# Expert stage of a two-block network: six row buffers in place of eight, and the last six query weight tiles loaded into a buffer of their own at the stage's beginning

## The reference, cut to what matters

```python
q = (x @ w_query).reshape(T, HEADS, 256)          # x: 256 x 1024, w_query: 1024 x 2048
s1 = einsum('thd,nd->thn', q[..., :128], sub_keys1)
s2 = einsum('thd,nd->thn', q[..., 128:], sub_keys2)
v1, i1 = top_k(s1, 16); v2, i2 = top_k(s2, 16)
top_s, top_p = top_k(all sums v1 + v2, 16)        # 16 experts of each head and token
e_idx = i1[top_p // 16] * 128 + i2[top_p % 16]
gate = softmax(top_s)
u = expert_u[e_idx]; act = gelu(einsum('cd,ced->ce', x, u))
y = einsum('ce,ced->cd', gate * act, expert_v[e_idx])
```

## Time and profile before

| | |
|---|---|
| Median of three executions | 2153.61 us (2153.51 to 2156.51) |
| The profiled execution's own time | 2153.96 us |
| Its span in the profile | 2152.2 us |
| PE, DVE, ACT, POOL busy over the span | 86%, 69%, 48%, 20% |
| Gathers | 256, together 268.45 MB |
| HBM read over the span | 494.73 MB, 230 GB/s in the mean |
| DMA rate in slices 9 to 19 of 40 (about 430 to 1020 us) | 416 to 422 GB/s |

### The profile page before, as it was taken

The page is one execution under the profiler, slowest core; times in us unless marked ns, Lnnn a source line. Parts: engine busy times, 40 slices in busy tenths (PEclk is TensorE's granted clock), DMA queues, the critical chain, the costliest instruction groups (busy, mean ns, idle before and its releaser), DMA issues. The chain is left out here.

```text
span 2152.2 us, 33416 instructions
## 1 busy us (share of the span) xinstructions
PE 1860.4 (86%) x12148; PEld 1393.9 (65%) x12148; DVE 1486.2 (69%) x2618; ACT 1026.3 (48%) x2065; POOL 436.7 (20%) x457
## 2 busy tenths in 40 slices
PE   4974897998987877777899989889999999779998
PEld 4842887844432222222289988678998989668997
DVE  6676654787777677666466675766777787777666
ACT  2444212554554444444355554467665545435554
POOL 0010220144544434444200000002221331210000
PEclk8987998899999999999999999799999999889999
DMA  9860001599999999999855555035555555224553
GB/s 333 290 224 35 3 3 41 187 416 420 421 421 421 422 421 421 421 420 422 358 178 187 185 179 198 1 118 184 187 182 180 190 181 176 93 91 158 192 186 98
DMA packets 104385, 497.31 MB, mean 231 GB/s; under 512 B 11856, under 2 KB 17232, under 8 KB 71376
## 3 DMA queue, kind: packets, MB, share of 16 engines
q1 hardware_dynamic: 66064, 225.41, 31.2%
q0 software_dynamic: 36864, 268.45, 30.0%
q10 hardware_dynamic: 1344, 1.96, 0.3%
HBM read 494.73 MB, written 1.05 MB: 230 GB/s over the span
## 5 line engine op out<-in xcount | busy, mean ns | idle before, releaser
L247 PE MATMUL ps<-srcs,wh 128*128 128x512 f32 x2064 | 742.1, 401 | 23.2 <-DVE srcs L261 20.4
L1924 PE MATMUL ps<-row,diag 128*128 128x512 f32 x1024 | 498.2, 622 | 114.5 <-ACT diag L2028 114.3
L249 PE MATMUL ps<-srcs,wl 128*128 128x256 f32 x2064 | 583.2, 283 | 0.0
L229 DVE TENSOR_TENSOR wl<-ring,wh 128x1024 fp32r<-128x1024 f32 x362 | 452.3, 1252 | 120.0 <-ACT wh L223 118.7
L247 PEld LDWEIGHTS ps<-srcs,wh 128*128 128x128 f32 x2064 | 392.6, 190 | 115.3 <-issue 27.2
L1924 PEld LDWEIGHTS ps<-row,diag 128*128 128x128 f32 x1024 | 183.0, 193 | 417.5 <-ACT diag L2028 258.9
L2129 DVE CUSTOM_DVE_ANT_0 row<-row,h_tok 128x1024 f32<-128x1024 f32 x256 | 313.5, 1225 | 191.7 <-DMA row<-in_peer_uv,experts 178.9
L223 ACT ACTIVATE wh<-ring 128x1024 fp32r<-128x1024 f32 x362 | 379.2, 1051 | 65.4 <-PE ps L249 43.1
L249 PEld LDWEIGHTS ps<-srcs,wl 128*128 128x128 f32 x2064 | 395.4, 192 | 2.5 <-issue 2.4
L1837 POOL DMA_INDIRECT row<-in_peer_uv,experts x256 | 280.5, 1096 | 384.2 <-PE ps L1924 346.7
L2021 ACT ACTIVATE acts<-dots 128x1 f32<-128x1 f32 x256 | 51.8, 202 | 328.4 <-DVE dots L2129 327.7
(11 more groups left out here) (520 smaller groups left out, 2180.3 us busy)
## 6 DMA issues: line engine op xcount, KB each, us to landing
ring<-in_stream SPq DMA_DIRECT2D x378, 512.0 KB, 3.8
alpha<-in_ada_late SPq DMA_DIRECT2D x12, 512.0 KB, 5.8
beta<-in_ada_late SPq DMA_DIRECT2D x10, 512.0 KB, 5.8
kappa<-in_ada_late SPq DMA_DIRECT2D x10, 512.0 KB, 6.3
row<-in_peer_uv,experts POOLq DMA_INDIRECT x256
bias<-in_attn_bias SPq DMA_DIRECT2D x8, 256.0 KB, 5.2
w<-in_cmp_w SPq DMA_DIRECT2D x1, 2048.0 KB, 7.7
xT<-in_xT SPq DMA_DIRECT2D x1, 1024.0 KB, 15.4
```

The lines of the kernel that those rows point to most:

```text
L229: nc.vector.tensor_tensor(wl[:, n % PAIRS, :], ring[:, tile % RING, :], wh[:, n % PAIRS, :].bitcast(F32), ALU.subtract).then_inc(tiles_fre ...
L247: nc.tensor.matmul(out, wh[:, n, cols], source.rearrange("p a t -> p (a t)"), start=start, stop=stop, skip_group_check=True)
L249: return nc.tensor.matmul(out[:, 0:S], wl[:, n, cols], source[:, 0, :], start=False, stop=stop, skip_group_check=True)
L1924: last = nc.tensor.matmul(y_part(t, half), diag[:, s % DIAGS, :], row[:, s % ROWS, D + half * 512:D + (half + 1) * 512], start=(slot == 0) ...
```

## The change

Six row buffers instead of eight free 16 KB in each partition. A new buffer `extra` with six places takes 24 KB; the difference is made up by letting `weights` share its memory with `dots` and `whole` with `hot`. At the stage's beginning, right behind the subkeys, SP loads query tiles 10 to 15 into `extra`. `refill` then loads only query tiles 6 to 9 into the ring; the six ring slots that tiles 10 to 15 would have had are skipped (SP waits for the slot's earlier load and counts its semaphore up itself), and the next stage's first two tiles are loaded as before, when query tiles 10 and 11 have been split. ACT and DVE read tiles 10 to 15 from `extra`. POOL's wait in front of gather s is now for `v_used` of slot s - 6.

```diff
-        def high(act, tile, turns=0):
+        def high(act, tile, turns=0, held=None):
 
             n = split_no(tile)
-            act.wait_ge(loaded[tile % RING], turns * 16 + 16 * (tile // RING + 1))
+            source = held[0] if held else ring[:, tile % RING, :]
+            if held:
+                act.wait_ge(held[1], 16)
+            else:
+                act.wait_ge(loaded[tile % RING], turns * 16 + 16 * (tile // RING + 1))
             if n >= PAIRS:
                 act.wait_ge(tiles_used, turns * RING + (n - PAIRS + 1))
-            nc.scalar.activation(wh[:, n % PAIRS, :], ring[:, tile % RING, :], ACT.Copy).then_inc(high_done, 1)
+            nc.scalar.activation(wh[:, n % PAIRS, :], source, ACT.Copy).then_inc(high_done, 1)
...
-        ROWS = 8
+        ROWS = 6
...
+        EXTRA = RING
         row_in = [sem(f"row_in{i}") for i in range(ROWS)]
+        extra_in = [sem(f"extra_in{i}") for i in range(EXTRA)]
...
-            whole = sb("query_whole", [P, 2, S], where=tmp)
+            extra = sb("extra", [P, EXTRA, D], where=tmp)
...
-            dots, acts, weights = (sb(n, [P, TT * SLOTS], where=tmp) for n in ("dots", "acts", "weights"))
+            dots, acts = (sb(n, [P, TT * SLOTS], where=tmp) for n in ("dots", "acts"))
+            weights = dots
...
+            whole = hot[:, :, :, :].rearrange("p a b c -> p a (b c)")
...
+            def extra_at(n):
+                return (extra[:, n, :], extra_in[n]) if 0 <= n < EXTRA else None
...
                 sp.dma_start(subkeys[:, :, :], A["subkeys"]).then_inc(keys_in, 16)
-                refill(sp, first, T_QUERY - RING + AHEAD)
+                for i in range(EXTRA):
+                    sp.dma_start(extra[:, i, :], A["stream"][first + T_QUERY - EXTRA + i]).then_inc(extra_in[i], 16)
+                refill(sp, first, T_QUERY - EXTRA - RING)
+                for i in range(T_QUERY - EXTRA, T_QUERY):
+                    slot = (first + i) % RING
+                    sp.wait_ge(loaded[slot], 16 * ((first + i) // RING))
+                    sp.sem_inc(loaded[slot], 16)
+                refill(sp, first + T_QUERY - RING, AHEAD)
                 for s in range(TT * SLOTS - ROWS, TT * SLOTS):
                     sp.wait_ge(row_in[s % ROWS], 16 * (s // ROWS + 1))
                 refill(sp, first + T_QUERY - RING + AHEAD, RING - AHEAD)
...
                 def weight_and_copy(i):
-                    high(act, first + AHEAD + i)
+                    n = AHEAD + i - (T_QUERY - EXTRA)
+                    high(act, first + AHEAD + i, held=extra_at(n))
                     copy_low(i)
```

More of the change, by code:

```diff
@@ L215, in split_no, with low @@
             return tile - T_ADA
-        def high(act, tile, turns=0):
+        def high(act, tile, turns=0, held=None):
             n = split_no(tile)
-            act.wait_ge(loaded[tile % RING], turns * 16 + 16 * (tile // RING + 1))
+            source = held[0] if held else ring[:, tile % RING, :]
[3 more added lines that the diff above has]
+                act.wait_ge(loaded[tile % RING], turns * 16 + 16 * (tile // RING + 1))
             if n >= PAIRS:
                 act.wait_ge(tiles_used, turns * RING + (n - PAIRS + 1))
-            nc.scalar.activation(wh[:, n % PAIRS, :], ring[:, tile % RING, :], ACT.Copy).then_inc(high_done, 1)
-        def low(dve, tile, turns=0):
+            nc.scalar.activation(wh[:, n % PAIRS, :], source, ACT.Copy).then_inc(high_done, 1)
+        def low(dve, tile, turns=0, held=None):
             n = split_no(tile)
+            source = held[0] if held else ring[:, tile % RING, :]
             dve.wait_ge(high_done, turns * RING + (n + 1))
-            nc.vector.tensor_tensor(wl[:, n % PAIRS, :], ring[:, tile % RING, :],
+            nc.vector.tensor_tensor(wl[:, n % PAIRS, :], source,
                                     wh[:, n % PAIRS, :].bitcast(F32), ALU.subtract).then_inc(tiles_freed, 1)
@@ L2146, in weight @@
                 def weight(i):
-                    low(dve, first + AHEAD + i)
+                    n = AHEAD + i - (T_QUERY - EXTRA)
+                    low(dve, first + AHEAD + i, held=extra_at(n))
                 def out(i):
```

## The result

The changed kernel takes **2162.63 us** in the median of nine executions (2158.43 to 2168.7). The kernel before, executed beside it, takes 2155.88 us (nine executions, 2153.51 to 2157.18). The ratio is 1.0036, with a 95% interval of 1.0026 to 1.0046. The change makes the kernel slower by some 7 us, where +1.1 us was forecast, and the time lies above the range given. The profiled execution of the changed kernel took 2160.01 us, 6.05 us more than that of before.

A forecast was written before the change was run, and what follows sets the result against it. The gathers' bytes on the DMA engines bound the stage; -6.2 us of tiles against about 8 us of dry queue came by the landings to +1.1 us, others 0: 2154.7 us, own range 2153.3 to 2155.1, wider range 2151.5 to 2158.5.

The forecast's parts named there:

- The bound: Expert stage's gathers: length is its bytes at 421 GB/s while the slowest DMA engine's queue never runs empty.
- The tiles, -6.2 us: Query tiles 11 to 15 leave the saturated stretch, 5 x 1.245 = 6.2 us, and cost nothing at the stage's beginning.
- The dry stretch, some 8 us: Stage's start: six gathers queued run dry at 432.6 us, gather 6 is issued at 439.88; engines idle some 8 us.
- An unqueued gather: Time from the end of its issue to its landing with nothing queued: taken as 4.2 us, bounds 3.4 and 4.6.
- The start, +1.1 us: Landing of gather 19 at 477.8 us against 476.75 before, tiles included: +1.1 us, bounds -0.3 and +1.5.
- gather k is now issued where gather k + 2 was: Rule for following landings after the dry queue: issues shift by two gathers while the consumers keep their times.
- The steady part, 0 us: After the start, a turn of six buffers lasts 14.9 us instead of 19.9; the slowest engine doesn't run dry: 0 us.
- that leaves 2.9 us, against 0.9 us from issue to first data: Gather 55, the tightest found: issue ends at 564.26 us, slowest engine begins it at 567.2, so it isn't starved.
- One sign named in the forecast: Prediction is wrong if dots in heads 1 to 4 wait over 2.49 us for each other in the mean.
- The slower one: Six buffers don't cover the loop; five tight gathers starve if issue to first data exceeds 2.9 us: 2159.7 us, chance 0.13.
- The faster rival: Slot 0 finishes earlier, queue isn't dry, the whole 6.2 us are gained: 2147.4 us, chance 0.08.
- The base: Starting time for the sum: profiled execution of the kernel before, 2153.96 us, with the median shown 0.35 us lower.

The follow-up runs named there:

- second profiles: The changed kernel and the kernel before, each executed and profiled again with no edit: changed 2161.6 us, ratio 1.0033; before against itself 0.9998.
- run 4: The kernel before with six row buffers instead of eight and no tile moved: 2163.14 us, ratio 1.0031.
- six behind the start: The kernel before, eight buffers kept, but gathers from the 33rd on wait as if there were six; tiles in place: 2159.21 us, ratio 1.0010.
- four under way: The kernel before, eight buffers kept, but from slot 80 on gather s also waits for gather s - 4 to land: ratio 1.0009.
- run 7: The kernel before, eight buffers kept, with at most four, three or two gathers under way from slot 80 on: ratios 1.0009, 1.029, 1.0729.
- Six at the start: The kernel before, eight buffers kept, but the first 32 gathers wait as if there were six; tiles in place: 2159.18 us, ratio 1.0014.

## Why the prediction was wrong

**The bound.** Right: the stage lasts as long as its bytes when the queue is full. Eight buffers with two tiles moved gained what they should, and the slowest engine decides: the last landing is still behind the rest. The tail is steeper, as forecast. The end of the gathers in the changed kernel, to be read beside the earlier trace rows:

```profile
1072.00:1075.00 3.00, 2.50 (x6) 0.68 (x4) 1.48 (x4) 1.11 (x5) 0.00 (x0) 1.00 0.99 412
1075.00:1078.00 3.00, 2.27 (x5) 0.68 (x4) 1.23 (x2) 1.38 (x5) 0.00 (x0) 1.00 0.23 96
```

Some 6 to 3 us ahead of the last dot the share is still 0.99; before it was 0.17 at that distance. The lag between the first and the last of the 16 engines at gather 255 is 3.2 us instead of 7.9 (2.1 instead of 8.1 in the second profiles).

**The tiles, -6.2 us.** Right as bytes: they are gone, and at their new place they delay nothing (0.61 of the DMA share from 392 to 415 us instead of 0.36, and the first gather follows the subkeys' issue by 22.9 us as before, 22.8). With six buffers at most 2.8 us of them are seen by slot 31, and in the medians nothing (run 4).

**The dry stretch, some 8 us.** Right in place and nearly in size. POOL's seventh gather waits 13.91 us, for PE, and is issued 22.13 us behind the first, 23.25 us in the second profile; forecast was 23.3. The row of the changed kernel for three us ahead of it:

```profile
439.00:442.00 3.00, 3.00 (x9) 1.33 (x8) 2.93 (x12) 1.14 (x5) 0.94 (x1) 1.00 0.01 3
```

The share is 0.01. (Forecast were 433 to 441 us; the whole stage began 2.9 us later.) In the mean of the 16 engines, idle time from the first issue to the landing of slot 19 grew by 6.7 and 7.6 us in the two pairs of profiles. An unqueued gather takes 4.50 us (gather 0) and 4.52 us (gather 6) from the end of its issue to its landing, where I took 4.2 of 3.4 to 4.6; over all the profiles gather 0 takes 4.50 to 4.81 us. From the Trainium skill, page "DMA: Bandwidth & Descriptors", section "Anatomy of one DMA — SWDGE (gpsimd) path", an estimate of 4.4 us was worked out. The trace agrees with it better than with my choice.

**The start, +1.1 us: the first step that failed.** It is +3.1 to +3.9 us. The missing term is the packets. From the point "gather k is now issued where gather k + 2 was", I took every packet behind the dry stretch at its duration in a full queue. With few gathers queued they aren't. Gather 6 lands 27.6 and 28.7 us behind the first issue in the two profiles of the changed kernel, where 28.5 was forecast. But from there to the landing of slot 19 it takes 36.6 and 36.0 us, where the forecast has 33.7. Of the packets of gathers 6 to 19, 33 and 3 took over 0.35 us in the two profiles of before, and 194 and 143 in those of the changed kernel. What the packets took over 0.312 us, spread over 16 engines, is 2.7 and 2.4 us more than before. With these the sum comes out: -6.2 us of tiles, 6.7 and 7.6 us of idle time and 2.7 and 2.4 us of packets make +3.2 and +3.8 us, where +3.1 and +3.9 us were measured. (Gathers 0 to 5 have 69 and 68 long packets too, against 27 and 25 before. They lie ahead of the dry stretch and only shorten it.)

There is also a slip in the forecast's own sum. Gather 15 was said to land at 467.3 us, "earlier than the queue lets it". From gather 11 on at 456.9 us the queue lets it at 456.9 + 4 x 2.49 = 466.9 us, so by the forecast's rule gather 15 decides, and the difference is +1.5 us, with +1.9 us as the upper bound. This moves the forecast by 0.4 us and is not why it failed; the bounds were too low because both ends held the same assumption about the packets.

**The steady part, 0 us: the second.** It is 0 in one profile of the changed kernel, 0 with six buffers and no tile moved, 3 us in the other changed profile and 3 us with six behind the start. The step that failed is "that leaves 2.9 us, against 0.9 us from issue to first data", with its end that the quicker engines may run dry for nothing. 0.9 us is when the first data flow, not when they flow at full speed. In the four profiles with six buffers behind the start the packets over 0.35 us go by the lead over the quickest engine: 13 to 21 of 128 in a gather with a lead under 1 us (two to four such gathers in a profile), 12 to 17 from 1 to 2 us, 3 to 9 from 2 to 3 us, 1 to 2 from 3 to 4 us, 0 to 1 above. Gathers 20 to 95 with a lead under 3 us: none in either profile of before, 12 and 22 in those of the changed kernel. The run with four under way has its quickest engine at 3.0 us and costs nothing. So a lead of 3 us over the quickest engine is enough, and 1.6 us isn't; my margin of 2.9 us was right in size (from gather 20 on the smallest is 2.9 us in each of the four profiles) but was counted on the slowest.

Two limits of this rule. No run lies between 1.6 and 3.0 us. And the quickest engine alone doesn't say it all: over all the runs, from gather 20 on, gathers with a lead of 2 to 3 us over the quickest engine have 13.1, 6.1, 2.9 and 0.3 long packets in the mean, as the lead over the slowest is 3 to 4, 4 to 5, 5 to 7 or over 7 us. The more of the 16 engines have a short lead, the more packets are long; the runs change both leads together and don't separate them.

What of the loss in the steady part reached the end was less than what the rate shows. In 480 to 640 us the two changed profiles lose 2.1 and 4.3 us of bytes, six behind the start 6.0 us. Part of this is no loss, as run 7 shows with its 417 GB/s. With the quicker engines held back, the slowest engine's lag shrinks, and its landings decide. From slot 95 to slot 255 six behind the start needs 399.7 us, against 402.3 before. This giving back is where "costs nothing" was half right.

One sign named in the forecast could not have shown any of it: dots in heads 1 to 4 further apart than 2.49 us in the mean. From slot 15 to slot 79 the landings are 2.57 and 2.58 us apart before and 2.56 and 2.58 us after.

**The rivals.** The slower one named the right kind of place (six buffers don't cover the loop, heads 1 to 4) and its 2159.7 us was near the 2160.01 us that the profile took, by luck: 2.9 us of the latter are chance ahead of the stage. Its mechanism was too narrow: it asked for the slowest engine to run dry, and its point of decision was wrong. The Trainium skill, page "Perfetto Trace Analysis", section "Identifying Performance Opportunities", was quoted for a repeated gap as the sign of too few buffers. The shortage was real here, and the sign hardly there: from 480 to 640 us the share was 1.01 and 1.00, and the rate fell to 416 and 410 GB/s. The faster rival needed a first free buffer at 432.6 us; it came 22.1 us behind the first gather, at the equivalent of 437.8 us, and 23.3 us in the second profile. That the dry queue can be avoided is shown by eight buffers.

**The base.** Of the distance between 2154.7 and 2162.63 us some 2.3 us aren't the change: the three executions shown of before had a median of 2153.61 us, nine have 2155.88, and the later comparisons have 2155.98 (30 executions), 2157.01 (25) and 2154.72 (12). I set the median 0.35 us below the profiled execution on the word of three.

**The account, and what is open.** Six at the start gives +0.14%, six behind it +0.10%, both with the tiles in place; together +0.24%, against +0.31% for six buffers whole and +0.36% and +0.33% for the change, with intervals of 0.1% on either side: the two parts make up the whole as far as these runs can tell. Between the profiles (+3.2 and +6.6 us) and the medians (+7 us) up to 4 us of the change aren't placed; chance between executions is of that size. It isn't shown what makes a packet long when the queue is short, nor whether it is the time of the lead or the number of gathers queued that counts. That the engine then fetches its next descriptors too late is a guess, for no row shows such a fetch.

## What to carry to other kernels

For a stage bound by gathers, count for each gather the lead between the end of its issue and the moment at which the quickest DMA engine could begin it; here 3 us are enough and 1.6 us are not, and a buffer is worth trying as long as it lifts some gather to 3 us. Move a transfer out of such a stage only where the queue is full at its time, and don't pay for it with buffers: two tiles moved and eight buffers kept beat both kernels. Judge a saturated stretch by its rate and by the time of a packet, not by the rounded busy share, and what it costs by the landings: 1% of the rate went for nothing in run 7.

## What the runs showed of the hardware

- DMA engines can be counted busy and still move less. At a share of 1.01 the rate from 480 to 640 us was 421, 416 or 413 GB/s, with 410 and 405 at 1.00. Some 40 to 50% of the difference is idle time that the rounded share hides. The rest lay in packets of 8 KB that took over 0.35 us (up to 1.7 and 2.0 us in the two profiles of the changed kernel) instead of 0.31. Behind an empty queue these are the first ones: at gathers 0 and 6 of the changed kernel 14 to 16 of the first 16.
- The price rises steeply as the lead falls. With a median of 3.0 us over the quickest engine (5.4 over the slowest) it is nothing, at 1.6 us (3.5) it is 0.32 us for a gather of 2.5 us, at 0.7 us (1.3) 0.87 us.
- The slowest of the 16 engines falls behind in steps of about 1 us, up to 7.9 us over the 256 gathers. Six of them, at the landings at 617.8, 688.3, 761.4, 822.0, 895.0 and 965.6 us of the kernel before, have the same two packets 1.5 to 2.4 us ahead: one of 8 KB of the kind `instruction` on queue `q14` (0.33 us), and 0.3 us behind its start a packet of the gathers that takes 0.96 to 0.97 us instead of 0.31. The second profile of before has the same six. The packets of 16 KB on `q8`, about 1.0 us long, don't go with the steps: those at 653.5 and 734.1 us lie 35 and 27 us ahead of the next one, and that at 971.5 us behind the last. That the packet on `q14` causes the step was not tried.
